# Split operand tensors of a one-core transformer kernel placed on multiples of 64 bytes

## The reference, cut to what matters

```
h = h + (mix @ w_out[l]).astype(h.dtype)
z = rms_norm_2(h, norm2_g[l])
h = h + jnp.square(jax.nn.relu(z @ w_mlp1[l])) @ w_mlp2[l]
```

## The kernel before, in words

| stage (time in the profile, us) | split operand | address | rest of address / 64 | rest / 128 |
|---|---|---|---|---|
| all | `w_hi`, `w_lo` | 32896, 41088 | 0 | 0 |
| attention and delta inputs (46 to 510) | `h_hi`, `h_lo` | 163264, 187840 | 0 | 64 |
| merge (837 to 1072) | `attn_back`, `h_lat`, `gdn_o`, hi and lo | 103872 to 185792 | 0 | 64 |
| out projection, first block (1072 to 1116) | `src_hi_buf`, `src_lo_buf` | 103872, 120256 | 0 | 64 |
| up (1126 to 1377), mixers, both first feed-forward products | `u_hi`, `u_lo` | 212960, 196576 | 32 | 96 |
| down (1377 to 1501) | `mid_hi`, `mid_lo` | 85472, 130528 | 32 | 96 |
| out projections of the second block (1690 and 2289) | `src_hi_buf`, `src_lo_buf` | 101856, 118240 | 32 | 96 |
| second feed-forward products | `mid2_hi`, `mid2_lo` | 85472, 118240 | 32 | 96 |

## Time and profile before

### The profile page before, as it was taken

How to read it: one execution, slowest core, us unless ns; L and a number is a source line. 1 busy time by engine, 2 the same in 40 slices (tenths; PEclk the granted TensorE clock), 3 DMA queues, 4 the chain that set the end, 5 groups by cost and what they waited for, 6 DMA issues and landing times.

```text
span 2713.4 us, 46124 instructions
## 1 busy us (share of the span) xinstructions
PE 2616.5 (96%) x19758; PEld 2079.9 (77%) x19758; DVE 1399.9 (52%) x1950; ACT 1023.2 (38%) x1697; POOL 277.2 (10%) x228
## 2 busy tenths in 40 slices
PE   7998999999998999899999999999999999999998
PEld 5754788778897788688888776788887876788886
DVE  4344698546777333566643546552453446552542
ACT  3245765333334323333333346322223355321222
POOL 0210102223420000111101001100001001100001
PEclk8999999989999999999999989999999999999999
DMA  6100310231004233222223211222222211222222
GB/s 260 59 17 16 113 61 26 80 127 50 4 4 148 93 100 125 77 94 93 94 91 95 86 47 47 93 93 94 93 94 93 86 40 56 93 93 94 93 94 70
DMA packets 64715, 222.90 MB, mean 82 GB/s; under 512 B 7168, under 2 KB 7552, under 8 KB 64384
## 3 DMA queue, kind: packets, MB, share of 16 engines
q1 hardware_dynamic: 63936, 218.38, 24.2%
q10 hardware_dynamic: 576, 1.57, 0.2%
HBM read 213.64 MB, written 6.29 MB: 81 GB/s over the span
## 4 chain that ended last, share of the span: by engine, by line
PE 88%; DVE 7%; issue 2%; ACT 2%; DMA 1%; POOL 0%; SPq 0%; POOLq 0%; DVEq 0%; ACTq 0%
PE ps L315 59%; PE ps L2690 6%; PE ps L1709 5%; PE ps L325 3%; PE ps L831 2%; PE ps L806 1%; PE ps L1734 1%; PE ps L1715 1%; PE ps L1751 1%; DVE w_lo L293 1%; PE ps L2741 1%; PE ps L2771 1%; PE ps L822 1%; DVE o_tok L1601 1%; DMA ring<-in_w_mod_first 1%
## 5 line engine op out<-in xcount | busy, mean ns | idle before, releaser
L293 DVE TENSOR_TENSOR w_lo<-ring,w_hi 128x1024 fp32r<-128x1024 f32 (+1 forms) x339 | 420.5, 1240 | 868.6 <-ACT w_hi L285 868.6
L285 ACT CAST w_hi<-ring 128x1024 fp32r<-128x1024 f32 (+1 forms) x339 | 353.2, 1042 | 954.5 <-PE ps L315 863.4
L315 PE MATMUL ps<-u_hi,w_hi 128*128 128x512 f32 x864 | 344.9, 399 | 8.7 <-DVE u_lo L574 8.7
L315 PE MATMUL ps<-u_lo,w_hi 128*128 128x512 f32 x864 | 343.1, 397 | 0.0
L315 PE MATMUL ps<-u_hi,w_lo 128*128 128x512 f32 x864 | 340.1, 394 | 0.0
L315 PE MATMUL ps<-mid_lo,w_hi 128*128 128x512 f32 x688 | 273.3, 397 | 0.0
L315 PE MATMUL ps<-mid_hi,w_hi 128*128 128x512 f32 x688 | 272.0, 395 | 0.0
L315 PE MATMUL ps<-mid_hi,w_lo 128*128 128x512 f32 x688 | 270.0, 393 | 0.0
L315 PEld LDWEIGHTS ps<-u_hi,w_hi 128*128 128x128 f32 x864 | 162.6, 188 | 53.0 <-issue 8.9
L315 PEld LDWEIGHTS ps<-u_hi,w_lo 128*128 128x128 f32 x864 | 162.7, 188 | 40.4
L315 PEld LDWEIGHTS ps<-u_lo,w_hi 128*128 128x128 f32 x864 | 162.8, 188 | 37.8 <-issue 0.5
(11 more groups left out here) (449 smaller groups left out, 4679.0 us busy)
## 6 DMA issues: line engine op xcount, KB each, us to landing
ring<-in_w_up SPq DMA_DIRECT2D x44, 512.0 KB, 3.4
ring<-in_w_in SPq DMA_DIRECT2D x42, 512.0 KB, 3.4
ring<-in_w_merge SPq DMA_DIRECT2D x32, 512.0 KB, 3.4
ring<-in_w_mlp1a SPq DMA_DIRECT2D x32, 512.0 KB, 3.4
ring<-in_w_mlp2a SPq DMA_DIRECT2D x32, 512.0 KB, 3.4
ring<-in_w_mlp1b SPq DMA_DIRECT2D x32, 512.0 KB, 3.4
ring<-in_w_mlp2b SPq DMA_DIRECT2D x32, 512.0 KB, 3.4
ring<-in_w_gdn_in SPq DMA_DIRECT2D x24, 512.0 KB, 3.5
```

The source lines that it names most:

```text
L285: nc.scalar.copy(w_hi[:, slot, 0:width], ring[:, n % RING, 0:width]).then_inc(*hi_ok.one())
L293: nc.vector.tensor_tensor(w_lo[:, slot, 0:width], ring[:, n % RING, 0:width], as_f32(w_hi[:, slot, 0:width]), ALU.subtract).then_inc(*lo_o ...
L315: mm = nc.tensor.matmul(dst[:, a:b], w[wi][:, k * P:(k + 1) * P], src[xi][:, k0 + k, a:b], start=start and k == wi == xi == 0, stop=stop a ...
```

## The change

Every tensor that `sbr` or `far_pair` allocates is asked for at a multiple of 64 bytes. `sb` is left as it is. No instruction is added, removed or moved.

```diff
+LINE = 64
...
         def sbr(ctx, name, *shape):
...
-            return ctx.enter_context(nc.sbuf_tensor(name, [P, *shape], F32R))
+            return ctx.enter_context(nc.sbuf_tensor(name, [P, *shape], F32R, align_bytes=LINE))
 
         def far_pair(ctx, name, *shape):
...
-            return tuple(ctx.enter_context(nc.sbuf_tensor(f"{name}_{part}{taken[name]}", [P, *shape], F32R, side="right"))
+            return tuple(ctx.enter_context(nc.sbuf_tensor(f"{name}_{part}{taken[name]}", [P, *shape], F32R, side="right",
+                                                          align_bytes=LINE))
                          for part in ("hi", "lo"))
```

## The result

Nine timed runs of each kernel: median 2712.1 us before (2706.9 to 2721.2), 2698.5 us after (2686.7 to 2706.4). The ratio is 0.9948, 95% interval 0.9928 to 0.9969, so the change saves 14 us, between 8 and 20. The forecast was 2684.3 us (2679 to 2692): the direction is right, the size is twice too large.

What follows compares the result with a forecast made beforehand. TensorE was taken as alone on the path. Moving operands 25.9 us plus stationary 1.7 us, together 27.6, less 0.6 for mixer waits, gave 27.0 us: from 2711.3 to 2684.3 us, range 2679 to 2692.

Steps and rivals of the forecast that it cites:

- The two paces: Out projection, first against second block: 228.8 against 233.3 ns per matmul, taken as 4.5 ns from operand placement.
- rival (c): Late stages: pace belongs to stages, not addresses, so nothing moves; 2711.3 us, chance 0.05.
- The change part by part: Late moving operands all become multiples of 64; 5760 matmuls gain 4.5 ns each, 25.9 us.
- The comparison of before: Kernel before: operands at multiples of 64 against operands 32 past one, 4.5 ns per matmul apart.
- The stationary term: Line 325, activation as stationary operand: 384 matmuls gain 4.5 ns each once at a multiple of 64, 1.7 us.
- Case (a): Late stages: only `u` gains, `mid`, `mid2` and late `src` keep 233.3 ns; 16.6 us won, 2694.7 us, chance 0.05.
- The Trainium skill's reading: SBUF lines of 16 bytes: a 32-byte shift crosses no line more or less, saving 0; given little weight.

Runs made afterwards that it cites:

- e1_all64: Changed kernel with `mid`, `mid2` and late `src` moved to start address 192 modulo 256, like `u`; median 2690.9 us, ratio 0.9926 to the kernel before.
- e4_after_again: The changed kernel once more, unaltered, for a second profile; median 2700.2 us, ratio 0.9955 to the kernel before.
- f3_fine: Weights at 128 modulo 256 as in the kernel before, late activations at distances 8, 16, 32, 80, 224 and 240 from them; 2710.6 us, one run.
- e2: Changed kernel with only `w_hi` and `w_lo` moved, to start address 192 modulo 256; 2680.7 us, one run.
- e3: Changed kernel with each late tensor at its own start address modulo 512, weights left at 128 modulo 256; 2707.5 us, one run.
- g2: Both weight halves at 128 modulo 256, hi and lo halves of the late activations at different start addresses; 2712.1 us, one run.
- f4: Kernel before, no 64-byte request, only `w_hi` and `w_lo` moved, to 224 modulo 256; median 2682.6 us, ratio 0.9887.
- f2_pairs: `w_hi` at 128 and `w_lo` at 64 modulo 256, most late activations' hi and lo halves placed apart; 2720.7 us, one run.
- f1_same_rest: Weights and all late activations at the same start address, 192 modulo 256; median 2677.1 us, ratio 0.9868 to the kernel before.

## Why the prediction was wrong

**Right.** TensorE's pace is what counts, and next to nothing hides it: the paces below add up to 17.3 us, and 17.5 appear between the first `u` and the end. `u` went to 228.8 ns, as forecast. The two paces were real, and addresses make them. Nothing up to 1116 us got another address, and rival (c) is out.

**The step that failed** is in "The change part by part": "All become multiples of 64", after which all 5760 matmuls are counted at 4.5 ns. The comparison of before holds one fast placement (distance 64) and one slow one (distance 96). A rule "multiples of 64 are fast" fits them, but so does every other rule that tells these two apart. The 3312 matmuls on `u` got the merge's distance of 64 bytes and gained 4.4 ns each, 14.6 us with the mixers' 720 counted in full. The 2448 on `mid`, `mid2` and late `src` got distance 128, which the kernel before had nowhere on line 315. On `mid` and `mid2` they gained 0.9 ns each (233.3 to 232.4), 1.9 us; the two late out projections, 40.18 us each on the chain before, took 40.02 and 40.18, 0.2 us less. That is 2.1 us instead of 11.0, and nearly all of the missing part of the sum. `e1_all64` puts it right by moving just these, and comes 6 us under the changed kernel in the late part (1562.9 against 1568.7 and 1569.4).

**The stationary term** was sized at 1.7 us. The first mixer's three pieces on line 325 take 22.71 us, 5.62 us and one of 5.80 more; after, they take 22.27, 5.61 and 5.79, which is 0.46 us less. In the second mixer the long piece took 22.83 before and 22.70 after, so 0.6 us came in all; in `e4_after_again` it took 22.3 in both mixers, which would make 1.0. Nearly all of it is in the piece with the 256-column matmuls. There the roles are swapped, so `u` at rest 192 under weights at 128 is distance 128 - 192 = -64, which is 192, a slow one for 512 columns (233.3 ns). So the 192 matmuls of 512 columns gained nothing, and the term was too high for that reason. What I read as the stationary operand's own alignment fits the same distance with its sign turned, though no run places line 325 on its own. The reading behind it was also looser than written: (22.71 - 48 x 0.2342) / 96 is 119.5 ns, or 117.8 with the last record taken off, so against 113.5 the difference is 4.3 to 6.0, not 4.5 to 5.

**The rivals.** Case (a), "only `u` gains", at 2694.7 us, is what happened, give or take the 0.9 ns of `mid`: 16.6 us against the 17.5 of the late part. I gave it 0.05 with this argument: the weights lie at multiples of 128, move at line 325, and run at 113.5 ns there. That argument was about an operand's own address, from 256-column matmuls, against a moving operand of 512 columns; it could not say anything on the distance. The chance was too low because the landing place of `mid` had no row, and the nearest row was of another shape. The sum 14.6 + 2.1 + 0.6 = 17.3 us agrees with the 17.5 of the first pair of profiles; the second pair has 1587.3 - 1568.7 = 18.6. The timed medians differ by 14 with an interval of 8 to 20, in which both lie; the first 1100 us, which alone differ by up to 9.5 us between the four profiles, can account for the rest.

The Trainium skill's reading ("SBUF — State Buffer", "Specifications (TRN2)": lines of 16 bytes) would have nothing change for a shift by a multiple of 32. The runs here contradict it: shifts by multiples of 32 change the pace by up to 7.5 ns (226.7 to 234.2).

**Still open** is the mechanism. In every trace the load of the next weights starts within some 10 ns of the matmul that streams, as in the changed kernel at 1850 us:

```profile
1850.04 0.39 PE L317 MATMUL ps<-mid_hi,w_hi 128*128 128x512 f32 x1
1850.04 0.19 PEld L317 LDWEIGHTS ps<-mid_lo,w_hi 128*128 128x128 f32 x1
1850.26 0.39 PE L317 MATMUL ps<-mid_lo,w_hi 128*128 128x512 f32 x1
1850.27 0.19 PEld L317 LDWEIGHTS ps<-mid_hi,w_lo 128*128 128x128 f32 x1
```

Two streams that set out together from addresses with a fixed distance could meet in the same part of the memory again and again. That would fit a dependence on distance with a period; it is argued, not shown, and the mixed placements don't follow from it. No run separated the two reads in time.

## What to carry to other kernels

Where TensorE alternates weight loads and float32r matmuls of 512 columns without a gap, put the stationary and the moving operand, hi and lo parts alike, at the same start address modulo 256; here it was worth 1.3%, or 1.1% with nothing but 512 bytes of padding around the weights, where the 64-byte request won 0.5%. When a natural experiment inside one profile shows two paces, write down every quantity that differs between its arms, differences of addresses included, and forecast only for places that one of the arms really has. Look at every shape that shares the weights: the best distance for 512 columns was among the slowest for 256 (next section). Read pace from start to start over a hundred matmuls, not from busy shares or from one timed run: the long runs repeated to 0.1% while the whole kernel scattered by 0.7%.

## What the runs showed of the hardware that was not expected

Pace per matmul of 512 columns (granted clock 1.00, the 2.4 GHz level) in the long stages, hi and lo parts of each operand placed alike, by distance:

| distance | ns | seen in |
|---|---|---|
| 0 | 226.7 | weights at 128, 192 and 224 |
| 8 | 232.5 and 233.3 | `f3_fine`, two stages |
| 16 | 231.7 | `f3_fine` |
| 32, 240 | 233.3 | `f3_fine` |
| 64 | 228.7 to 229.1 | both kernels, `e1`, `e2`, `e3`, `g2` |
| 80 | 231.3 | `f3_fine` |
| 96 | 233.3 | kernel before |
| 128 | 232.4, and 233.3 in one stage | changed kernel, `e3_places` |
| 160 | 234.2 | `e3_places` |
| 192, 224 | 233.3 | `e3_places`, `f3_fine`, `f4` |

The address is not all of it: at the same addresses a stretch can have one of two paces. This holds for the two rows of 8 and 128 above, whose stages of 384 matmuls differ by 0.8 to 0.9 ns at one address, and for `u` in `f2_pairs` with both halves at rest 64, 233.3 ns in one half of the layer and 231.1 in the other. The largest step is at distance 64. In `e1_all64` the two late out projections have the same distance, 64, and the same code:

```profile
L333 PE MATMUL ps<-src_hi_buf,w_hi x47: 388/388/389, 1689.8 to 1721.4; 128*128 128x512 f32 x47
...
L333 PE MATMUL ps<-src_hi_buf,w_hi x42: 397/397/398, 2284.8 to 2313.5; 128*128 128x512 f32 x42
```

31.6 / 138 = 229.0 ns in the first, 28.7 / 123 = 233.3 in the second. And 144 matmuls of line 325 that took 16.34 us in the first profile of the kernel before took 16.97 in its second:

```profile
56.85 16.97 PE ps L325 x144
```

That is 113.5 and 117.8 ns per matmul, a step of the same 4.4 ns; whether it is the same effect is open. This is part of the scatter between executions. No long run at distance 0 was seen in a slower pace, which may be why that placement won as much as it did; the profiles are too few to call it shown. At distance 0 matmuls of 256 columns on line 325 are slower, not faster (17.28 us for the 144, `f1_same_rest`), so the best distance depends on the shape:

```profile
56.95 17.28 PE ps L345 x144
```
